# Sixteen expert buffers in one ring, four experts per loop turn, and overflow blocks of 32 tokens on four column tiles

## The reference

```python
logits = (xt @ w_router + b_router)
top_logits, top_idx = lax.top_k(logits, 4)          # 256 tokens x 4 = 1024 slots, 32 experts
top_w = softmax(top_logits)
# per expert e, on the tokens that chose it:
gate, up = split(xb @ w_gu[e] + b_gu[e], 2)          # w_gu[e]: 1024 x 2048
gate = minimum(gate, 7.0); up = clip(up, -7.0, 7.0)
act = (up + 1) * (gate * sigmoid(1.702 * gate))
y[tok] += (act @ w_dn[e] + b_dn[e]) * top_w          # w_dn[e]: 1024 x 1024
```

## Time and profile before

| | us |
|---|---|
| runs of the kernel before (median of 3) | 2118.11 (2112.33 to 2120.79) |
| profiled execution, its own time | 2111.71 |
| profiled execution, span | 2110.0 |
| TensorE busy / DVE / ACT | 1948.9 / 908.0 / 469.5 |
| TensorE, gate and up of main blocks (L1182, 64 records each) | 459.2 |
| TensorE, down projection (L1220) | 258.3 |
| expert stage, first bias to last scatter | 362.58 to 1383.66 |
| mean granted TensorE clock | 0.98 |

### The profile page before, as it was taken

One profiled execution on the slowest core, in us unless ns is written; L12 is line 12 of the kernel. 1 busy time (PEld: TensorE's weight loads), 2 busy tenths in 40 slices (PEclk: granted clock), 3 DMA queues, 4 the chain that ended last, 5 costly groups with the idle time before them and its releaser, 6 DMA issues. The chain is left out here.

```text
span 2110.0 us, 28553 instructions
## 1 busy us (share of the span) xinstructions
PE 1948.9 (92%) x10917; PEld 1222.1 (58%) x10918; DVE 908.0 (43%) x1444; ACT 469.5 (22%) x557; POOL 70.5 (3%) x128
## 2 busy tenths in 40 slices
PE   4999896999999999999999999989999998999998
PEld 2859774433333333333333333358987997878986
DVE  3799644111111111111111121176556787876554
ACT  2223101000000000100000000024543643334542
POOL 2000002000000000000000000010000000020000
PEclk9999997999999999999999999999999989999999
DMA  9794834959999999899999985936555620054552
GB/s 360 246 324 156 300 126 146 417 216 422 421 422 422 422 422 422 332 423 422 422 422 422 408 344 226 401 107 213 180 198 164 202 96 1 1 173 162 189 190 80
DMA packets 143604, 581.37 MB, mean 276 GB/s; under 512 B 10520, under 2 KB 12552, under 8 KB 94281
## 3 DMA queue, kind: packets, MB, share of 16 engines
q1 hardware_dynamic: 136384, 564.43, 68.6%
q0 software_dynamic: 3040, 11.02, 1.7%
q10 hardware_dynamic: 4105, 4.86, 0.7%
HBM read 579.23 MB, written 1.05 MB: 275 GB/s over the span
## 5 line engine op out<-in xcount | busy, mean ns | idle before, releaser
L1182 PE MATMUL bank<-ring,area 128*64 128x512 f32 x2048 | 459.2, 597 | 28.0 <-DMA ring<-in_w_gu 27.6
L1182 PEld LDWEIGHTS bank<-ring,area 128*64 128x64 f32 x2048 | 144.0, 137 | 325.3 <-issue 235.5
L924 PE MATMUL bank<-area_r,ring_r 128*128 128x256 f32 x992 | 282.6, 285 | 9.3 <-DVE area_r L2155 7.1
L926 PE MATMUL bank<-area_r,ring_r 128*128 128x256 f32 x992 | 281.5, 284 | 0.0
L927 PE MATMUL bank<-area_r,ring_r 128*128 128x256 f32 x992 | 281.5, 284 | 0.0
L289 DVE TENSOR_TENSOR ring_r<-ring,ring_r 128x2048 fp32r<-128x2048 f32 x90 | 205.8, 2291 | 149.8 <-ACT ring_r L286 148.1
L2420 DVE TENSOR_SCALAR area<-bank 128x512 f32<-128x512 f32 x36 | 24.9, 692 | 539.6 <-PE bank L1182 539.6
L286 ACT ACTIVATE ring_r<-ring 128x2048 fp32r<-128x2048 f32 x92 | 175.7, 1913 | 179.4 <-PE bank L927 152.2
L924 PEld LDWEIGHTS bank<-area_r,ring_r 128*128 128x128 f32 x992 | 191.3, 193 | 12.1 <-DVE area_r L2155 7.3
L1220 PE MATMUL bank<-area 128*64 128x512 f32 x864 | 192.5, 594 | 0.6 <-DVE area L2434 0.5
L926 PEld LDWEIGHTS bank<-area_r,ring_r 128*128 128x128 f32 x992 | 191.3, 193 | 0.0
(11 more groups left out here) (341 smaller groups left out, 2177.8 us busy)
## 6 DMA issues: line engine op xcount, KB each, us to landing
ring<-in_w_gu SPq DMA_DIRECT2D x256, 1024.0 KB, 21.1
area<-in_w_dn SPq DMA_DIRECT2D x96, 1024.0 KB, 21.0
ring<-in_mlp_w SPq DMA_DIRECT2D x64, 1024.0 KB, 5.4
ring<-in_w_dn SPq DMA_DIRECT2D x32, 1024.0 KB, 19.5
ring<-in_w_in SPq DMA_DIRECT2D x24, 1024.0 KB, 6.3
ring<-in_gdn_w_in SPq DMA_DIRECT2D x16, 1024.0 KB, 5.5
area<-in_w_mod SPq DMA_DIRECT2D x12, 1024.0 KB, 8.6
ring<-in_w_mod SPq DMA_DIRECT2D x8, 1024.0 KB, 17.1
```

Source lines behind the costliest of these rows:

```text
L924: ins = mm(out_, a_[0], b_[0], start=start, stop=False)
L926: mm(out_, a_[0], b_[1], start=False, stop=False)
L1182: ins = mm(bk[hf * BLK:(hf + 1) * BLK, :], x(kt), block_u[:, c:c + BANK], start=False, stop=kt == ND - 1)
```

## The change

Three things change together.

The buffers become one ring in order of use: load n goes to buffer n mod 16 and the order is gate and up, then down, expert by expert. As 12 loads an expert and 16 buffers meet again only after four experts, a loop turn now holds four (`EG = 4`), while tokens are still gathered for pairs (`EPAIR = 2`). The rule by which a load waits is unchanged.

An overflow block now has 32 tokens (`OBLK`). Its inner loop runs over blocks 2 to 7 (`Fori(OVER0, OVER1)`). Gate and up, bias and down are written anew for it: each quarter of the columns (256) goes to one of four column tiles of 32; the activation is 128 x 256 instead of 128 x 512.

Main blocks count the same twelve uses. The loads ahead of the next stage wait for other counts: ring buffers 0 to 3 are free once expert 30 is done, and the two small loads (and one of POOL's) wait until expert 31's gate and up is used, since their places are now part of the ring to the end.

```diff
-EG = 2
+OBLK = 32
+EG = 4
+EPAIR = 2
...
-PE_OVER = ("gathered", "gate_up", "scattered", "spread_T", "act_T0", "act_T1", "down")
+PE_OVER = ("gathered", "gate_up", "scattered", "spread_T", "act_T", "down")
...
+    OVER0, OVER1 = BLK // OBLK, S // OBLK
...
-        GU_SLOTS = tuple(range(NGU))
-        DN_SLOTS = ((8, 9, 10, 11), (12, 13, 14, 15))
...
-        ER = NU + len(DN_SLOTS[1])
+        ER = 16
+        assert EG * NU % ER == 0
...
         def expert_slot(j, u):
-            return GU_SLOTS[u] if u < NGU else DN_SLOTS[j][u - NGU]
+            return (NU * j + u) % ER
...
-        load_order = [(0, u) for u in range(NGU)] + [(0, u) for u in range(NGU, NU)]
-        for e in range(1, NE):
-            load_order += [(e, u) for u in range(NGU, NU)] + [(e, u) for u in range(NGU)]
+        load_order = [(e, u) for e in range(NE) for u in range(NU)]
...
-                    with eng.Fori(1, NBLK) as b:
-                        with eng.If(n_tok - b * BLK > 0):
+                    with eng.Fori(OVER0, OVER1) as b:
+                        with eng.If(n_tok - b * OBLK > 0):
                             overflow((g, j, b))
                         with eng.Else():
...
-                    sp.wait_ge(w_used, PRE + NU * (NE - 1) + s + 1)
+                    sp.wait_ge(w_used, PRE + NU * NE - ER + s + 1)
...
-            sp.wait_ge(w_used, PRE + NU * (NE - 1))
+            sp.wait_ge(w_used, PRE + NU * (NE - 1) + NGU)
...
+            def over_gate_and_up(w):
+
+                for kt in range(ND):
+                    block_u = weights(w, kt)
+                    for part, bk in ((0, bG), (1, bU)):
+                        for q in range(4):
+                            c = part * D + q * (D // 4)
+                            ins = mm(bk[q * OBLK:(q + 1) * OBLK, 0:D // 4], xg_o[:, kt, :], block_u[:, c:c + D // 4],
+                                     start=False, stop=kt == ND - 1)
+                step(ins)
...
+            def over_down(w):
+
+                DV.did(pe, w, "act_T")
+                for n, v in enumerate(DN_ORDER):
+                    block_u = weights(w, NGU + n)
+                    for k in range(2):
+                        for hf in range(2):
+                            r, c = (2 * hf + k) * OBLK, k * D + hf * BANK
+                            ins = mm(bT[r:r + OBLK, :], actT[:, k, v * OBLK:(v + 1) * OBLK],
+                                     block_u[:, c:c + BANK], start=n == 0, stop=n == 3)
+                step(ins)
```

More of the change, by code:

```diff
@@ L598, in did @@
                 else:
-                    eng.wait_ge(self.sem, g * self.per + b * self.over_len + (base - self.over_len + self.over[step]))
+                    eng.wait_ge(self.sem, g * self.per + b * self.over_len + (base - OVER0 * self.over_len + self.over[step]))
             def started(self, eng, where, less=0):
@@ L662, in _ @@
                 s = expert_slot(e % EG, u)
+                assert s == n % ER
                 if n >= ER:
@@ L1173, in gate_up_bias, with gate_and_up @@
                            start=True, stop=False)
-            def gate_and_up(w, x, last):
+            def gate_and_up(w, x):
                 for kt in range(ND):
@@ L1209, in spread_transposed, with down @@
                 step(ins)
-            def down(w, last):
+            def down(w):
                 for n, v in enumerate(DN_ORDER):
@@ L1262, in overflow @@
                 spread_transposed(w, spread)
-                activation_T(w, 0, bG)
-                activation_T(w, 1, bU)
-                down(w, False)
+                over_activation_T(w)
+                over_down(w)
             def last_block(w):
@@ L1282, in last_block @@
                 spread_transposed(w, spread)
-                down(w, True)
+                down(w)
             pe.wait_ge(moe_act, 3)
@@ L1789, in act_block @@
                 DV.did(act, w, "gate_min")
-                f(g_sig, g_min, ACT.Sigmoid, scale=SWIGLU).then_inc(moe_act, 1)
-                if isinstance(w[2], int) and w[1] == EG - 1:
+                wide = BANK if isinstance(w[2], int) else D // 4
+                f(g_sig[:, 0:wide], g_min[:, 0:wide], ACT.Sigmoid, scale=SWIGLU).then_inc(moe_act, 1)
+                if isinstance(w[2], int) and w[1] % EPAIR == EPAIR - 1:
                     f(xg[0], xg_staged, ACT.Copy).then_inc(moe_act, 1)
@@ L2396, in find_slots @@
             def find_slots(dst, e, b):
-                row = slot_row[:, 0, 0, :] if isinstance(b, int) else \
-                    slot_row[:, bass.ds(b, 1), 0, :].rearrange("p o s -> p (o s)")
+                row = main_row[:, 0, :] if isinstance(b, int) else \
+                    over_row[:, bass.ds(b, 1), :].rearrange("p o s -> p (o s)")
                 for t in range(NT):
@@ L2468, in last_block @@
                 PE.started(dve, w)
-                if j == 0:
-                    for i in range(EG):
-                        find_slots(slots[:, :, i * BLK:(i + 1) * BLK], e + (EG + i), 0)
+                if j % EPAIR == 0:
+                    for i in range(EPAIR):
+                        find_slots(slots[:, :, i * BLK:(i + 1) * BLK], e + (j + EPAIR + i), 0)
                 find_spread(spread, e + j, 0)
-                limited(w)
-                gated(w)
+                limited(w, BANK)
+                gated(w, BANK)
                 PE.did(dve, w, "next_gathered")
-                copy_tokens(xg_staged if j == 0 else xg[1])
+                copy_tokens(xg_staged if j % EPAIR == 0 else xg[1])
                 expert_row(e + (j + 1))
```

106 lines of the change are left out of this document (60 added, 46 removed).

## The result

| | kernel before | kernel after |
|---|---|---|
| median of the runs, us | 2117.7 | 2423.7 (2418.2 to 2431.5) |
| ratio, 95% interval | | 1.145 (1.1405 to 1.150) |
| span of the profiled execution, us | 2110.0 | 2429.8 |
| expert stage, first bias to last scatter | 362.58 to 1383.66: 1021.1 | 370.98 to 1698.42: 1327.4 |
| mean granted TensorE clock | 0.98 | 0.90 |

The kernel is 306 us slower, more than twice what was forecast (142) and far outside the range (up to 2288). The stage alone accounts for all of it: 1327.4 - 1021.1 = 306.3. The rest of the difference between the two profiled spans, 13.5 us, lies outside it: the first bias starts 8.4 us later, behind the first expert's own empty turns (with six turns alone it starts at 371.25 too), and 5.1 us come behind the last scatter.

A forecast was written before the change was run, and what follows sets the result against it. TensorE bounds about 19 experts, DMA 13. Changed, TensorE rules: 851 base, 0.8 end, 3.8 cold start, 94 turns, 40 clock, 60 code, 93 overflow, 20 gaps: 1163 us against 1021, +142, forecast 2260, range 2160 to 2288.

The forecast's parts named there:

- +84: Whole kernel: the forecast change if code stays resident and everything else is as forecast, 2202 us.
- ring and order: Expert weight loads: sixteen buffers and the same wait rule, only the order differs; worth zero.
- code term: TensorE's loop body, 1,182 to 2,872 instructions: code fetched anew at branches each turn, 9.1 us a turn, 60 us taken.
- upper: TensorE's loop code: no piece survives a turn, eight turns at 9.1 us are 73, less savings 60; lower bound 2.
- Whether code stays: TensorE's loop: six pieces are held, the new body spans twelve, so code was taken not to stay.
- Turns: Ahead of main blocks: three more empty overflow-loop turns of 1.12 us lie bare on TensorE, 3.35 us each time, 94 us.
- Clock: Behind the new idles ahead of main blocks: TensorE's clock falls, 1.3 us a time, 27 + 4 times, 40 us.
- Small blocks: Overflow blocks: five of 32 tokens at 18.6 us, 93 in all, instead of four of 64 at 31.1 each.
- (c): Overflow blocks: four tiles don't run side by side at 256 columns, 6.8 us more each; +176, 2294 us; chance 0.09.
- (a): TensorE's loop: the code stays resident, everything else as forecast; +84, 2202 us; chance 0.25.
- (b): TensorE in the expert stage: resident code and a clock that never falls; +44, 2162 us; chance 0.08.
- (d): TensorE's queue: empty turns stay covered, DMA rules again between overflows; -18, 2100 us; chance 0.08.

The follow-up runs named there:

- light_loads: The kernel after with each expert weight load cut to its first 256 of 2048 columns; 2333.0 us, ratio 1.102.
- small_blocks_only: The kernel after with the loop, buffers and load order of the kernel before, keeping 32-token overflow blocks and six turns; 2235.1 us, ratio 1.056.
- outer_if_two: The kernel before with 32-token overflow blocks on four column tiles and one outer If around the inner loop; 2130.6 us, ratio 1.007.
- pad_2180: The kernel before with 250 never executed matmuls at the end of the loop body; 2124.2 us, ratio 1.004.
- first_block_apart: The kernel before with the first 64-token overflow block behind one If and the further two behind a second If within it; 2381.1 us, ratio 1.126.
- two_pads: The kernel before with 250 never executed matmuls behind each of the loop body's two experts; 2534.0 us, ratio 1.197.
- four_experts_only: The kernel before with four experts per loop turn and nothing else; 2235.8 us, ratio 1.056.
- ring_only: The kernel before with one ring of sixteen buffers, loads in order of use and four experts per loop turn; 2233.5 us, ratio 1.055.
- outer_if_four: The kernel after with one outer If that skips the inner loop for experts of up to 64 tokens; 2241.4 us, ratio 1.061.
- outer_if_before: The kernel before with one outer If around its inner loop, 64-token blocks kept; 2113.7 us, ratio 0.999.
- six_turns: The kernel before with an inner loop of six turns instead of three; 2249.3 us, ratio 1.063.
- block_last: The kernel before with one outer If and its inner-loop turns in opposite order, empty turns ahead of the overflow block; 2127.8 us, ratio 1.006.

## Why the prediction was wrong

Direction and place were right and every loss forecast was found, and the time was wrong by 164 us. Read as a ladder of kernels, each step with its own run:

| step | forecast, us | measured, us |
|---|---|---|
| turns and clock (six turns, alone) | part of the +84 | +132 (stage +130.7) |
| small blocks in place of large ones | part of the +84 | -14 (stage -15.8) |
| ring and order | 0 | 0 (2233.5 beside 2235.8) |
| body of 2,872 instead of 1,446 instructions | +60 | +189 (stage +191.4) |
| sum | +142 | +306 |

**The step that failed is the code term.** I put a branch into the next piece at 1.5 us, one over one and a half pieces at 1.9, and nine microseconds on a turn of the loop. These came from the miss of 2.14 us in the first pass of before. That trace also holds the reason why it is so short: the packet of code starts before 387.6, 0.3 us ahead of the branch at 387.87. The DMA queues of the kernel before from 387.0 to 387.55, then from 387.0 to 387.6:

```profile
q1 hardware_dynamic: 32, 0.24, 103.0%
```

```profile
q1 hardware_dynamic: 34, 0.25, 100.9%
q8 instruction: 1, 0.02, 11.2%
```

Here too the branch ended 2.4 us after the packet had begun. It waited for the rest of a fetch that had run ahead, and 2.14 is not the price of a fetch. The price is 3.5 us on idle queues and 6 behind the loads (light_loads), and at each turn of the loop 6.4 more at the closing branch. A turn of the loop with four plain experts thus waits some 28 us for code, not 9. In the kernel after the 27 long branches of the If last 146 us more than 0.2 each and the seven closing ones 43: 189 in all, beside the 191 by which the stage grew in this step. How many would miss was right: 98 more fetches, where about a hundred were forecast. The bound called "upper" only asked how many branches miss; the price of one miss had a single row under it and no upper end but the 16 us for "slower fetches".

**Whether code stays: right, for a reason that was too coarse.** The argument was that "nothing larger than six pieces was ever seen to stay". The runs set the limit: after first passes of six (before), seven (small_blocks_only, outer_if_two) and eight pieces (pad_2180) nothing is fetched again; where a turn touches more, all of them are fetched in every turn, nine (first_block_apart), ten (two_pads), eleven (four_experts_only) and thirteen (the kernel after). The Trainium skill, "Runtime: NRT & Kernel Launch", Instruction fetch mechanics, gives TensorE 2,048 instructions in pieces of 256, a FIFO, with the next piece fetched while one is executed. These runs agree with the eight pieces, and with the following piece being fetched; that nine keep none fits a FIFO. The forecast treated its second rule (a taken branch is cheap only within two pages) as refuted by the branch of 0.208 us over the whole old body; that stands, and 0.208 over 8.5 pieces in the padded kernel adds to it.

**Turns: right.** 1.12 to 1.14 us a turn, and the three further ones bare: 3.1 to 3.5 us of idle. In the stage of the run with six turns 1151.8 us stand beside the 1147 that its expectation had worked out.

**Clock: right in kind, too small.** I took 1.3 for a fall, "as not every one need fall". All fell, many for longer than the rows of before had shown, and plain experts of small_blocks_only take 32.0 us on average: 26.6 + 3.35 + 2.1. That is 0.8 x 28 = 22 us of the 33 by which the forecast without code (+84) fell short of the measured one (+117 by the medians). In the kernel after the low clock covers 380 us of the stage, in the one before 4.

**Small blocks: rate right, its price in clock not seen.** The four tiles do run side by side at 256 columns, so rival (c) is out. Where the clock was up throughout, in outer_if_two at expert 2, gate and up of an overflow block took 7.11 us, the 7.1 of the sum. In the kernel after it took 9.5, since the clock fell ahead of it. TensorE's timeline of outer_if_two (L1211) and the windows of small_blocks_only in the same place show both:

```profile
423.92 7.11 PE L1211 MATMUL bank<-ring,apad 128*32 128x256 f32 x128 [0.27 <-DVE apad L2509]
```

```profile
442.20:446.20 4.00, 4.00 (x40) 1.97 (x44) 0.00 (x0) 0.00 (x0) 0.00 (x0) 0.50 0.71 297
448.20:451.70 3.50, 3.50 (x70) 1.80 (x58) 0.00 (x0) 0.00 (x0) 0.00 (x0) 1.00 0.00 0
```

Of the matmuls as the trace records them, 40 start in 4 us at 1.2 GHz and 70 in 3.5 us at 2.4.

**The rivals.** (a) and (b) needed resident code and (d) covered turns; none came. (d) had also priced what the change was to bring if it worked, -18 us. outer_if_two is close to that case, without the ring and the longer body, and it is +0.7%: the two blocks of expert 16 cost 18.6 us more of standstill, twice the 9 that (d) allowed.

**What stays open.** Why the clock was low in the overflow block of expert 2 in the kernel after, with no idle ahead of its gather of 32-column matmuls, and not in outer_if_two at the same place, was not tried apart. And whether a piece is dropped by the order of fetching or by the order of use can't be told from these runs, since in a turn of nine both drop all.

## What to carry to other kernels

Count the pieces of code that one turn of a loop touches, with the next piece behind each, and keep them within what has been seen to stay; code that is never executed counts when it lies between what is. A price for a miss must come from a row in which the fetch starts after the branch, under the same DMA load: a short miss in a first pass is the rest of a fetch that had started before. And when control flow is added, ask whether TensorE's queue has room for it: three empty turns were free, six cost 6%.

## What the runs showed of the hardware

- A branch of TensorE's queue to code that isn't there lasts 3.5 us with DMA queues nearly idle (light_loads) and about 6 behind 1 MB loads (the kernel after). With q1 at 101.7% the packet of code, itself about 1 us long, came 3.5 us after the branch had begun.
- Eight pieces of 16 KB stay from turn to turn (pad_2180, 2124 us), nine don't (first_block_apart, 2381 us), and code that is jumped over counts: with the skipped block of pad_2180 standing twice in the body the time is 2534 us (two_pads).
- From the second expert on, TensorE's clock stayed up after every idle of 1.54 to 1.82 us ahead of a main block's bias (the kernel before, four_experts_only, ring_only, outer_if_four), did either at 1.85 to 1.90 (outer_if_before, ring_only) and was low behind every one of 1.98 and more (four_experts_only, outer_if_four, six_turns). Of four idles of 2.32 to 2.45 ahead of a gather three brought it down (block_last).
- Matmuls of 128 x 32 by 256 columns on four column tiles start every 0.055 us, as the trace records them, over a whole block (128 in 7.1 us) at full clock (outer_if_two, expert 2).
